# Down projection of a hybrid decoder step: three plain token pairs instead of two, and the sum units moved

## The reference

```python
x = x + g2 * ((jax.nn.silu(u) * val) @ p['w_down'])     # (2048, 2816) @ (2816, 1024)
y_prompt = rms_norm(x, final_w)
```

## Time and profile before

| | us |
|---|---|
| median of 3 runs | 2731.04 (2729.42 to 2732.64) |
| profiled execution, its own time | 2730.92 |
| span of the profiled execution | 2729.0 |
| TensorE busy | 2477.2 (91%) |
| VectorE busy | 1868.3 (68%) |
| ScalarE busy | 910.3 (33%) |
| mean granted TensorE clock (1 is 2.4 GHz) | 0.951 |

### The profile page before, as it was taken

The page is one execution under the profiler, slowest core; times in us unless marked ns, Lnnn a source line. Parts: engine busy times, 40 slices in busy tenths (PEclk is TensorE's granted clock), DMA queues, the critical chain, the costliest instruction groups (busy, mean ns, idle before and its releaser), DMA issues. The chain is left out here.

```text
span 2729.0 us, 44581 instructions
## 1 busy us (share of the span) xinstructions
PE 2477.2 (91%) x17104; PEld 1523.5 (56%) x17104; DVE 1868.3 (68%) x3831; ACT 910.3 (33%) x1383; POOL 403.4 (15%) x384
## 2 busy tenths in 40 slices
PE   3899999789999998699879999999999978889997
PEld 1455555467677776455446666666666643334443
DVE  4555556447788877478767777777777666677766
ACT  1433434114444444144422222222222233232222
POOL 0122323200000000022331222122221200000000
PEclk6999999889999999699989999999999999989999
DMA  7434443551242313233321222212222135443333
GB/s 257 156 105 149 165 133 104 164 169 34 106 148 92 116 58 97 65 126 113 116 70 62 62 72 78 74 53 74 72 78 69 54 116 186 153 135 100 109 89 93
DMA packets 209320, 291.36 MB, mean 107 GB/s; under 512 B 19727, under 2 KB 146239, under 8 KB 207027
## 3 DMA queue, kind: packets, MB, share of 16 engines
q1 hardware_dynamic: 208933, 289.72, 32.5%
q10 hardware_dynamic: 270, 0.10, 0.0%
HBM read 214.48 MB, written 75.29 MB: 106 GB/s over the span
## 5 line engine op out<-in xcount | busy, mean ns | idle before, releaser
L2586 PE MATMUL py<-h_parts,w_heads 128*128 128x384 f16 (+1 forms) x792 | 246.1, 311 | 19.6 <-DVE u_p L2741 19.6
L2587 PE MATMUL py<-h_parts,w_heads 128*128 128x384 f16 (+1 forms) x792 | 245.8, 310 | 0.0
L2588 PE MATMUL py<-h_parts,w_heads 128*128 128x384 f16 (+1 forms) x792 | 245.8, 310 | 0.0
L336 PE MATMUL prj<-w_heads,h_parts_t 128*128 128x512 f16 x512 | 196.0, 383 | 12.4 <-PEq L451 6.2
L337 PE MATMUL prj<-w_heads,h_parts_t 128*128 128x512 f16 x512 | 195.8, 382 | 0.0
L338 PE MATMUL prj<-w_heads,h_parts_t 128*128 128x512 f16 x512 | 195.6, 382 | 0.0
L336 PE MATMUL m_prj<-m_h,w_heads 128*128 128x128 f16 (+1 forms) x1088 | 179.7, 218 | 11.6 <-DMA m_h<-h_parts 10.3
L2586 PE MATMUL px<-h_parts,w_heads 128*128 128x384 f16 (+1 forms) x528 | 164.4, 311 | 17.5 <-PEq L1884 17.5
L337 PE MATMUL m_prj<-m_h,w_heads 128*128 128x128 f16 (+1 forms) x1088 | 179.6, 218 | 0.0
L338 PE MATMUL m_prj<-m_h,w_heads 128*128 128x128 f16 (+1 forms) x1088 | 179.6, 218 | 0.0
L336 PE MATMUL d_pm<-d_w,w_heads 128*128 128x512 f16 x392 | 154.0, 393 | 27.0 <-DVE w_heads L2450 27.0
(11 more groups left out here) (553 smaller groups left out, 6027.5 us busy)
## 6 DMA issues: line engine op xcount, KB each, us to landing
C_new<-in_w_up_dram SPq DMA_DIRECT2D x11, 2048.0 KB, 7.5
w_heads<-in_w_up_dram SPq DMA_DIRECT2D x44, 512.0 KB, 5.5
d_a<-act_cols SPq DMA_DIRECT2D x174, 128.0 KB, 2.5
act_cols<-w_heads SPq DMA_DIRECT2D x44, 384.0 KB, 2.4
win_raw<-in_w_ada_dram SPq DMA_DIRECT2D x8, 2048.0 KB
first_a<-in_w_down_dram SPq DMA_DIRECT2D x22, 512.0 KB, 3.9
first_a<-in_w_down_dram SPq DMA_DIRECT2D x44, 256.0 KB, 3.3
wa<-in_w_ada_dram SPq DMA_DIRECT2D x4, 2048.0 KB, 11.3
```

The costliest lines, as they stand in the source:

```text
L336: nc.tensor.matmul(out, left[0], right[0], start=(k == 0), stop=False)
L2586: nc.tensor.matmul(out, left[0], right[0], start=(start and k == 0), stop=False, skip_group_check=True)
L2587: nc.tensor.matmul(out, left[0], right[1], start=False, stop=False, skip_group_check=True)
L2588: last = nc.tensor.matmul(out, left[1], right[0], start=False, stop=(k == KC // 2 - 1), skip_group_check=True)
```

## The change

- `PLAIN` is 3: pairs 0, 1 and 2 are plain. Pair 2 uses the PSUM banks of pair 0, and its first step waits until these are emptied; `FIRST` and the counts in `bank_free` follow, and `plain_scale` runs for pairs 1 and 2 at j = 0 of the next pair.
- The units are at steps 11 to 32. In VectorE's step `unit_work` comes last. ScalarE cuts a unit's high part in the step after its sums (`unit_hi(n - 1)`), behind `cut_a_hi` of that step. SP loads unit u in its step u + 13 instead of u + 9. Its wait is, as before, for the sums of unit u - 1, which are now made at the end of VectorE's step u + 10.
- A fourth raw buffer for weights (`RAW` has 0 to 3, the semaphores and `dn.raws` too); ScalarE's wait at block 9 is for nine blocks instead of eight.
- In step 1 VectorE runs `lo_own(1)` ahead of `turn_w(2)`. The search for the activations' largest value is spread out: `fold_rows` at step 4 instead of 2, the matmul of `spread_rows` at TensorE's step 6 instead of 4, `power_of_two` at step 9 instead of 4.
- `plain_scale(0)` stays at step 13, `plain_scale(1)` moves from 13 to 15.

```diff
@@ -2287,11 +2287,11 @@
     J = FB // 2
-    RAW = (0, 0, 1, 2, 0, 1, 2, 0, 1, 2, 1)
+    RAW = (0, 0, 1, 2, 3, 0, 1, 2, 0, 1, 2)
     W_OF = (1, 3, 2, 6, 4, 5, 0)
     A_OF = (1, 2, 6, 0, 3, 4, 5)
-    PLAIN = 2
-    UNITS, UNIT_AT = 2 * J, 8
+    PLAIN = 3
+    UNITS, UNIT_AT = 2 * J, 11
     OF_PLAIN = (((0, 1), (1, 3)), ((4, 2), (0, 0)), ((2, 1), (3, 3)), ((5, 2), (2, 0)))
@@ -2303,7 +2303,7 @@
         self.src_a = core.aT.rearrange("(h f) p t -> f p h t", h=2)
-        self.w_in = [core.sem(f"d_w_in{i}") for i in range(3)]
+        self.w_in = [core.sem(f"d_w_in{i}") for i in range(4)]
         self.a_in = [core.sem(f"d_a_in{i}") for i in range(4)]
@@ -2939,7 +2939,7 @@
         work = sb("d_work", [P, 6 * D])
-        dn.raws += [work[:, 0:2 * D], work[:, 2 * D:4 * D]]
+        dn.raws += [work[:, 2 * n * D:2 * (n + 1) * D] for n in range(3)]
         dn.tsum = work[:, 5 * D:5 * D + 768].rearrange("p (q n) -> p q n", q=3)
@@ -2962,8 +2962,8 @@
         PAIRS, N = NCH // 2, J * (NCH // 2)
-        ORDER, FIRST = (0, 5, 1, 6, 4, 3, 2), (0, 1, 3, 2, 5, 6, 4)
-        banks = ((pm[:, 0], pm[:, 1], pm[:, 2], pm[:, 3]), (pm[:, 5], pm[:, 6], pm[:, 4], aux[:, 0:512]))
+        ORDER, FIRST = (0, 5, 1, 6, 4, 3, 2), (5, 6, 4, 0, 1, 2, 3)
+        banks = ((pm[:, 0], pm[:, 1], pm[:, 2], pm[:, 3]), (pm[:, 5], pm[:, 6], pm[:, 4], aux[:, 0:512]), (pm[:, 0], pm[:, 1], pm[:, 2], pm[:, 3]))
         y_rows = io["y_prompt"][0].rearrange("(c p) n -> c p n", p=P)
@@ -2978,7 +2978,7 @@
             def unit_for(n):
-                u = dn.unit(n - 1)
+                u = dn.unit(n - 2)
                 if u is not None:
@@ -3021,7 +3021,7 @@
                 if i < dn.PLAIN:
-                    pe.wait_ge(s["emptied"], {0: 2, 1: 4, 2: 4, 3: 4, 5: 5, 6: 6, 4: 7}[m])
+                    pe.wait_ge(s["emptied"], {5: 5, 6: 6, 4: 8, 0: 9, 1: 10, 2: 11, 3: 12}[m])
                 elif m in (0, 4):
@@ -3033,6 +3033,8 @@
                 a, w = dn.a_parts(n), dn.slot(j)
+                if i == 2 and j == 0:
+                    pe.wait_ge(s["emptied"], 4)
                 for bank, pair in zip(banks[i], dn.OF_PLAIN):
@@ -3069,7 +3071,7 @@
                     tops.turn_rows(pe, 2)
-                if n == 4:
+                if n == 6:
                     tops.spread_rows(pe, 2)
@@ -3101,18 +3103,18 @@
                 if j == 9:
-                    act.wait_ge(dn.w_lo, 8)
+                    act.wait_ge(dn.w_lo, 9)
                 if j == 10:
 ...
                 dn.cut_a_hi(act, j)
-                unit_hi(j)
+                unit_hi(j - 1)
             for n in range(J, N):
 ...
                     keep(i - 1)
-                unit_hi(n)
+                unit_hi(n - 1)
                 if j == 3:
@@ -3165,7 +3167,7 @@
                     if k > 1:
-                        dve.wait_ge(s["saved"], 32)
+                        dve.wait_ge(s["saved"], 32 * i)
                     ins = nc.vector.scalar_tensor_tensor(out=out_of(k)[:, half], in0=banks[i][2 * r + t], scalar=ks[:, group(i):group(i) + 1], in1=g_p[:, half],
@@ -3203,18 +3205,22 @@
                 if u is not None:
+                    if u == 0:
+                        dve.wait_ge(dn.w_lo, 5)
                     dn.sums_unit(dve, u)
 ...
             for j in range(1, J):
-                if j + 1 < J:
+                if 1 < j < J - 1:
                     dn.turn_w(dve, j + 1)
                 dn.lo_own(dve, j)
+                if j == 1:
+                    dn.turn_w(dve, 2)
                 dn.sums_a(dve, j + 1)
 ...
                 unit_work(j)
-                if j == 2:
+                if j == 4:
                     tops.fold_rows(dve, 2, steps)
-                if j == 4:
+                if j == 9:
                     power_of_two(nc, steps, tops.result(dve, 2)[:, 0:2], core.mscale[:, 2:4], core.minv[:, 2:4], bits[:], 2)
@@ -3223,7 +3229,7 @@
                 dn.cut_a_lo(dve, n)
-                if j == 0 and i == dn.PLAIN:
+                if j == 0 and 1 < i <= dn.PLAIN:
                     plain_scale(2 * i - 2)
@@ -3231,10 +3237,10 @@
                     scale(2 * i - 2)
-                unit_work(n)
                 if n == J + 2:
 ...
                     plain_scale(0)
+                if n == J + 4:
                     plain_scale(1)
@@ -3248,6 +3254,7 @@
                     norm(2 * i - 1)
+                unit_work(n)
             scaled = core.mscale[:, 3:4]
 ...
             nc.vector.scalar_tensor_tensor(out=dec[:, 1, 0:2].rearrange("p h f t -> p h (f t)"), in0=dec_raw, scalar=scaled,
```

## The result

The changed kernel takes **2702.88 us** (median of 4 runs, 2701.89 to 2703.06) against 2731.84 for the kernel before beside it: a ratio of 0.9893 with a 95% interval of 0.9876 to 0.991, 29 us faster. 2704 was predicted, with a range of 2692 to 2719. The profiled execution took 2702.91 us, its span is 2701.1, its mean granted clock 0.957 (before 0.951).

A forecast was written before the change was run, and what follows sets the result against it. VectorE's late `cut_a_lo` was taken to starve TensorE before 2444.02 us. Step 33 was to start at 2430.2 instead of 2457.6, 27.4 us less: 2730.9 - 27.4 = 2703.5, as a median 2704 us, range 2692 to 2719.

The forecast's parts named there:

- The start: Step 1: `lo_own(1)` moved into VectorE's idle time cuts TensorE's gap from 3.7 to some 1.6 us; the clock holds.
- Steps 2 to 10: First pass: without units VectorE's 4.2 us stay below TensorE's 5.18; step 11 at 2299.1, bringing 14.8 us up to there.
- The first unit: Unit 0, loaded last of a queue, lands at 2299.9; `cut_a_lo(12)` at some 2301.8, early enough for step 12.
- The loop: Single unit buffer (sum, issue, land, sum): sums 5.46 to 6.76 us apart before, longer than TensorE's 5.18; the loop stays.
- Steps 12 to 32: VectorE sets the pace; the 21 intervals from `cut_a_lo(12)` to `cut_a_lo(33)` sum to 126.0 us.
- light steps: The 13 unit steps counted without extra cost for scales, norm or x: 5.6 us each, 72.8 in all.
- The end: After `cut_a_lo(33)`: plain scale, last unit and cut, so step 34 starts at 2434.7 and TensorE is full again.
- The fourth buffer: Fourth raw weight buffer lets block 4 load at once and later blocks a step sooner; counted at zero.
- Rival 1: Units share the queue, so all 13 light steps take 6.76 us: + 15, 2719 us; chance 0.20 for 2712 to 2725.
- Rival 2: Units land within 3.8 us, all 22 steps cost TensorE's 5.18: 2686.4 us; chance 0.10 for 2680 to 2695.
- Rival 3: First pass not freed: late blocks, or constants and unit 0 hold the second pass; 2729 to 2733, no change; chance 0.03.
- Rival 4: Steps 12 to 32: gaps in every step drop the clock to 1.2 GHz, about 2800 us; chance 0.04.

The follow-up runs named there:

- the start undone: The changed kernel with `turn_w(2)` ahead of `lo_own(1)` in step 1 again: 2705.05 us, ratio 0.99.
- two unit buffers: The changed kernel with a second buffer for odd units, so a unit's load waits for the sums of the last unit but one: 2687.37 us, ratio 0.9838.
- the order undone: The changed kernel with unit work ahead of the rows again and ScalarE cutting a unit's high part in its own step: 2706.93 us, ratio 0.9912.
- only the units moved: The kernel before with one number changed, units at steps 10 to 31 instead of 8 to 29: 2723.2 us, ratio 0.9969.
- two plain pairs: The changed kernel with two plain pairs instead of three and units at steps 10 to 31: 2700.91 us, ratio 0.9892.

## Why the prediction was right

- **The start** came as worked out. Step 1 began at 2247.05 (2246.7 predicted), after a gap of 2.05 us instead of 1.6, and the clock held. With the start undone, the gap of 4.16 was followed by slow products, but the whole was worth 2 to 3 us.
- **Steps 2 to 10** ran without a gap, and VectorE's 4.2 us per step stayed below 5.18. Step 11 began at 2299.60 (2299.1 predicted), ten steps of 5.18 and 0.7 for the two small matmuls (0.5) behind 2247.05. The gain up to there is 14.3 us (14.8). The reason named for it, that steps 8 to 10 have no units, is **one way to it and not needed**: the units moved by themselves bring step 11 forward by 9.5 us, but with units at 8 the rest of the change brings 13.8 of the 14.3. The prediction saw the first way alone.
- **The first unit** landed for sums at 2299.70 (2299.9), and `cut_a_lo(12)` ran at 2301.29 (2301.8).
- **The loop:** The earlier trace rows are the first sums of units 10 to 13, not 14 to 17, and don't stand for all steps: from 2314 to 2444 VectorE waited for 8 of 19 units, 3.9 us in all, and for the other 11 the unit had landed. In the kernel before the loop was not yet what most steps waited for; after the change it is (16 waits, 30.4 us), as two unit buffers show.
- **Steps 12 to 32:** `cut_a_lo(33)` ran 2427.32 - 2301.29 = 126.0 us later, as predicted, with errors that cancel. The 13 light steps, from unit to unit, took 75.5 instead of 72.8: eleven took 5.2 to 5.9, and two, behind a save and a load of x, 6.7 and 6.9. The steps with norm were 6.5 each (6.8), as the square cost 0.78 instead of 1.0. The two of j = 5 took 5.5 and 5.6 (6.35), because x was there or 0.6 us late:

```profile
2326.57 1.22 DVE L3185 TENSOR_TENSOR d_work<-d_work 128x1024 f32<-128x1024 f32 x1
2392.80 1.23 DVE L3185 TENSOR_TENSOR d_work<-d_work 128x1024 f32<-128x1024 f32 x1 [0.60 <-DMA d_work<-x_mid]
```

- **The end:** step 34 began at 2434.21 (2434.7), and TensorE was full from there.
- **The fourth buffer** was counted at zero; it is worth 0.7 us, which the runs don't tell from zero.
- **Rival 1** (units share the queue) holds in two of 13 steps. One detail against it was wrong: `load_a` is not issued 2.3 us ahead of the unit but right behind it, as SP's queue shows:

```profile
2301.07 1.20 SPq L2364 DMA_DIRECT2D first_a<-in_w_down_dram  x2
2302.33 1.10 SPq L2405 DMA_DIRECT2D d_a<-act_cols  x2
```

- **Rival 2** (TensorE keeps up) gave 2686.4 for a unit that is always in time. That is what two unit buffers measure, 2687.4.
- **Rival 3** fell: the first pass is free. It had as well named too many loads at once; the first stretch moves 248 GB/s, and behind step 1 no step of it waits.
- **Rival 4** (the clock falls in the plain steps), the slower side, fell: 16 gaps of 0.16 to 1.52 us in steps 12 to 34 leave every product at 0.38 or 0.39 us. The Trainium skill, page "TensorE: Matmul & The Clock Gate", section "A second HAM failure mode: psum-queue depth-cycling", holds that frequent short idle spells make the clock swing; for gaps of this length the trace after the change does not agree, while the kernel before and the order undone do swing behind gaps of 2.43 us and more. What the prediction missed is that the kernel before had this loss all along: it counted the slow products behind steps 1 and 9 only, not the six later spells, because it went by the times at which steps began. The sum was not harmed, since it runs from one start to another; the account of where the gain comes from was.

The parts do not add up to 29 us. Undone one at a time, the start costs 2.2, the order 4.0, the buffer 0.7, the units' place and the third pair nothing. The intervals of these ratios overlap that of the changed kernel; 2.2 and 4.0 rest on runs that lie apart, by 0.2 and 2.0 us. Each leaves the others in place, and the first pass shows how one can cover for another: the units' place by itself frees most of it, and the rest of the change without the units' place nearly all. That all of them work in this way, against gaps ahead of TensorE's steps that are long enough for slow products to follow, is not shown: combinations of two edits undone were not tried, nor was the spread search for the largest value undone. In the kernel before VectorE stood 1.89 us for that search in step 4, and a gap of 0.75 us ahead of step 5 of TensorE followed; after the change that gap is gone.

## What to carry to other kernels

A load, a use and a wait through a single buffer are a loop with a period of its own (here 1.3 us for the sums, some 3.9 to 4.6 for issue and landing, 5.4 and 5.6 behind a save). Compare that period with the step of the engine that should set the pace: with a loop of 5.2 to 5.9 against 5.18, rearranging left 15.5 us, which a second buffer then took. Where an engine waits for a load, look on the issuing queue for what that load stood behind; here unit 0's waited for a buffer that it doesn't use. In each step put the work that nobody waits for last, and judge an order by its longest gaps too, not only by their sum: two kernels with the same idle time differed by 24 slow products.

## What was not expected

Slow products follow only the longer gaps, with no sharp line between. In all traces of this case, no gap of up to 2.05 us in the stage was followed by products of 0.6 us, every one of 2.43 us and more was, and in between it went either way: 2.17 and 2.21 were (only the units moved), 2.33 (before) and 2.42 (two plain pairs) were not. A spell of slow products costs 1.4 to 2.7 us, which comes on top of the gap.
